# First-layer recurrence: scores ahead of the key transposes, fillers dropped, keys and two joins moved from VectorE to ScalarE

## The reference, cut to what matters

```
z = p[..., (2 + d) * A_WIDTH:(3 + d) * A_WIDTH]
f = max(lb[d] + (1 - lb[d]) * sigmoid(z), F_MIN)
log_f = log(f);  k = 1 - f
# per chunk:
b = cumsum(gc)
decay[t, s] = exp(min(b[t] - b[s], 0)) where s <= t, else 0
scores = einsum('bhtk,bhsk,bhtsk->bhts', qc, kc, decay)
out = (q * exp(b)) @ state + scores @ v
new_state = exp(b_last) * state + (k * exp(b_last - b)).T @ v
```

## Time and profile before

| | before |
|---|---|
| median of 3 runs | 2728.24 us (2727.13 to 2730.35) |
| the profiled execution's own time | 2725.84 us |
| its span, first to last instruction | 2724.0 us |
| TensorE busy in the span | 2551.5 us (94%) |
| VectorE busy | 1672.8 us (61%) |
| ScalarE busy | 992.0 us (36%) |
| mean granted TensorE clock | 0.986 of full speed |

### The profile page before, as it was taken

One profiled execution on the slowest core, in us unless ns is written; L12 is line 12 of the kernel. 1 busy time (PEld: TensorE's weight loads), 2 busy tenths in 40 slices (PEclk: granted clock), 3 DMA queues, 4 the chain that ended last, 5 costly groups with the idle time before them and its releaser, 6 DMA issues. The chain is left out here.

```text
span 2724.0 us, 36802 instructions
## 1 busy us (share of the span) xinstructions
PE 2551.5 (94%) x14963; PEld 2155.6 (79%) x14963; DVE 1672.8 (61%) x2730; ACT 992.0 (36%) x1361; POOL 86.9 (3%) x132
## 2 busy tenths in 40 slices
PE   7999988999999999988999999998989988989997
PEld 2888877888888888866679989976678886767786
DVE  4888875457677766544446756746666775354744
ACT  4226544432211222344344323324542223434632
POOL 0110000000000000000000000002100000000000
PEclk9999999999999999999999999999999999999999
DMA  6650002223344333221013443321220001211232
GB/s 237 192 165 26 17 16 78 80 76 93 99 147 127 100 107 103 78 70 49 1 55 116 132 155 121 121 84 54 78 72 16 16 9 39 97 55 66 76 103 85
DMA packets 62106, 232.28 MB, mean 85 GB/s; under 512 B 6897, under 2 KB 9585, under 8 KB 61298
## 3 DMA queue, kind: packets, MB, share of 16 engines
q1 hardware_dynamic: 46962, 175.40, 19.5%
q0 software_dynamic: 14976, 54.53, 6.4%
HBM read 227.02 MB, written 2.10 MB: 84 GB/s over the span
## 5 line engine op out<-in xcount | busy, mean ns | idle before, releaser
L378 DVE TENSOR_TENSOR w_lo<-w_raw,w_hi 128x1024 fp32r<-128x1024 f32 (+4 forms) x284 | 348.7, 1228 | 376.1 <-ACT w_hi L337 370.6
L337 ACT ACTIVATE w_hi<-w_raw 128x1024 fp32r<-128x1024 f32 (+4 forms) x284 | 297.8, 1049 | 222.7 <-PE late_acc L459 93.4
L459 PE MATMUL mid_acc<-mid_h_hi,w_hi 128*128 128x258 f32 x832 | 279.4, 336 | 1.5 <-DVE mid_od_fq L627 1.0
L459 PE MATMUL mid_acc<-mid_h_hi,w_lo 128*128 128x258 f32 x832 | 279.0, 335 | 0.0
L459 PE MATMUL mid_acc<-mid_h_lo,w_hi 128*128 128x258 f32 x832 | 277.1, 333 | 0.0
L459 PE MATMUL late_acc<-late_h_hi,w_hi 128*128 128x258 f32 x704 | 199.3, 283 | 0.0
L459 PE MATMUL late_acc<-late_h_hi,w_lo 128*128 128x258 f32 x704 | 198.4, 282 | 0.0
L459 PE MATMUL late_acc<-late_h_lo,w_hi 128*128 128x258 f32 x704 | 197.7, 281 | 0.0
L459 PEld LDWEIGHTS mid_acc<-mid_h_hi,w_hi 128*128 128x128 f32 x832 | 157.3, 189 | 19.3 <-issue 2.4
L459 PEld LDWEIGHTS mid_acc<-mid_h_lo,w_hi 128*128 128x128 f32 x832 | 157.5, 189 | 18.6 <-issue 1.2
L459 PEld LDWEIGHTS mid_acc<-mid_h_hi,w_lo 128*128 128x128 f32 x832 | 156.8, 189 | 16.1
(11 more groups left out here) (552 smaller groups left out, 6126.6 us busy)
## 6 DMA issues: line engine op xcount, KB each, us to landing
w_raw<-in_up SPq DMA_DIRECT2D x88, 512.0 KB, 3.6
mid_side_raw<-in_ada_t POOLq DMA_DIRECT2D x48, 512.0 KB, 3.9
w_raw<-in_down SPq DMA_DIRECT2D x32, 704.0 KB, 4.0
qvz_side_raw<-in_ada_t POOLq DMA_DIRECT2D x32, 512.0 KB, 4.5
w_raw<-in_dn_qkv SPq DMA_DIRECT2D x25, 512.0 KB, 3.3
late_side_raw<-in_ada_t POOLq DMA_DIRECT2D x24, 512.0 KB, 4.2
w_raw<-in_da SPq DMA_DIRECT2D x18, 512.0 KB, 3.3
w_raw<-in_ev_qvz SPq DMA_DIRECT2D x16, 512.0 KB, 4.3
```

The lines of the kernel that those rows point to most:

```text
L337: nc.scalar.activation(K.whi[:, g % 2, 0:width], K.raw[:, g % 2, 0:width], ACT.Copy).then_inc(K.hi_done, 1)
L378: nc.vector.tensor_tensor(K.wlo[:, g % 2, 0:width], K.raw[:, g % 2, 0:width], K.whi[:, g % 2, 0:width].bitcast(F32), ALU.subtract).then_in ...
L459: last = nc.tensor.matmul(self.acc[i % len(self.acc)][:, at:at + width], left[:, j, cols], right[k][:, moving:moving + width], start=(k == ...
```

## The change

Four things change, all in the class `Recurrence`:

- On TensorE `turn_keys` goes from ahead of the scores (turn 5) to behind `base_scores` (turn 7), and `BUSY_KEYS` keeps only the 10 fillers of unit 0.
- On ScalarE `keys_back` goes from turn 6 to turn 7, behind a new stage `place`, which writes the parts of the two largest joins (128 and 64) into `S` by three plain copies; `merge` on VectorE keeps the two small joins and the base part.
- The keys `1 - f` are made by ScalarE at the head of `log`, from a bias of ones, and no longer by VectorE.
- On VectorE `update` stands ahead of `both`.

```diff
-    BUSY_KEYS = {0: 10, 4: 18, 5: 2, 7: 18, 8: 2, 9: 9, 10: 8, 11: 8}
+    PLACED = 2
+    MERGES = len(JOINED) - PLACED + 1
+
+    BUSY_KEYS = {0: 10}
...
-        def keys(n):
-            if n >= 2:
-                dve.wait_ge(self.mixed, n - 1)
-            nc.vector.tensor_scalar(self.heads(self.k[n % 2]), self.of_z(n), -1.0, 1.0,
-                                    ALU.mult, ALU.add).then_inc(self.k_done, 1)
...
-            if n >= 2:
-                dve.wait_ge(self.o_done, n - 1)
-            for l, size in enumerate(JOINED):
-                if l % 2 == 0:
-                    dve.wait_ge(self.scored, 3 * n + l // 2 + 1)
-                if l:
-                    dve.wait_ge(self.merged, 5 * n + l)
+            dve.wait_ge(self.placed, n + 1)
+            dve.wait_ge(self.scored, 3 * n + 2)
+            for l in range(self.PLACED, NL):
+                size = JOINED[l]
+                if l > self.PLACED:
+                    dve.wait_ge(self.merged, self.MERGES * n + l - self.PLACED)
...
-        yield from self.turns({0: [(0, merge)], 1: [(1, decayed_base)], 2: [(1, decayed)], 3: [(3, keys)],
-                               4: [(0, both), (0, update)], 5: [(2, base_and_ends)], 6: [(2, levels)], 7: [(3, sums)]})
+        yield from self.turns({0: [(0, merge)], 1: [(1, decayed_base)], 2: [(1, decayed)],
+                               4: [(0, update), (0, both)], 5: [(2, base_and_ends)], 6: [(2, levels)], 7: [(3, sums)]})
...
         def log(n):
+            if n >= 2:
+                act.wait_ge(self.mixed, n - 1)
+            nc.scalar.activation(self.heads(self.k[n % 2]), self.of_z(n), ACT.Identity, scale=-1.0,
+                                 bias=self.K.ones[:, 0:1]).then_inc(self.k_done, 1)
             act.wait_ge(self.k_done, n + 1)
             nc.scalar.activation(self.of_z(n), self.of_z(n), ACT.Ln).then_inc(self.logged, 1)
...
+        def place(n):
+            d = n % 2
+            if n == 0:
+                act.wait_ge(self.zeroed, 1)
+            if n >= 2:
+                act.wait_ge(self.o_done, n - 1)
+            act.wait_ge(self.scored, 3 * n + 1)
+            for l in range(self.PLACED):
+                size = JOINED[l]
+                nb, h = CHUNK // size, size // 2
+                late, early = self.late(d, size)
+                out = self.heads(self.S[d]).rearrange("p h (n e) -> p h n e", e=size)
+                at = l * A_HEADS * (CHUNK // 2)
+                got = self.ps_s[0][:, at:at + A_HEADS * (CHUNK // 2)].rearrange("p (h n e) -> p h n e", h=A_HEADS, e=h)
+                for m in range(nb):
+                    keys = slice(m * size + early.start, m * size + early.stop)
+                    last = nc.scalar.activation(out[keys, :, m, late], got[keys, :, m, :], ACT.Copy)
+            last.then_inc(self.placed, 1)
...
-                               6: [(1, keys_back)]})
+                               6: [(1, place)], 7: [(1, keys_back)]})
...
             if n:
-                pe.wait_ge(self.merged, 5 * (n - 1) + 2 * half + 2)
+                if half == 0:
+                    pe.wait_ge(self.placed, n)
+                else:
+                    pe.wait_ge(self.merged, self.MERGES * (n - 1) + NL - self.PLACED)
...
-        yield from self.turns({2: [(0, read_out)], 3: [(0, gain)], 5: [(1, turn_keys), (1, lambda n: scores(n, 0))],
-                               6: [(1, lambda n: scores(n, 1))], 7: [(1, base_scores)]})
+        yield from self.turns({2: [(0, read_out)], 3: [(0, gain)], 5: [(1, lambda n: scores(n, 0))],
+                               6: [(1, lambda n: scores(n, 1))], 7: [(1, base_scores), (1, turn_keys)]})
```

More of the change, by code:

```diff
@@ L1115, in __init__ @@
          self.mixed, self.scored, self.merged, self.k_turned, self.kt_done, self.o_done, self.o_taken, self.u_done,
-         self.updated) = K.signals("gl", "loaded zeroed k_done logged summed related grown ends mixed scored merged "
-                                   "k_turned kt_done o_done o_taken u_done updated")
+         self.updated, self.placed) = K.signals(
+             "gl", "loaded zeroed k_done logged summed related grown ends mixed scored merged "
+             "k_turned kt_done o_done o_taken u_done updated placed")
     SLOTS = range(-3, 12)
-    BUSY_KEYS = {0: 10, 4: 18, 5: 2, 7: 18, 8: 2, 9: 9, 10: 8, 11: 8}
+    PLACED = 2
+    MERGES = len(JOINED) - PLACED + 1
+    BUSY_KEYS = {0: 10}
     def at(self, n):
@@ L1263, in merge @@
             dve.wait_ge(self.scored, 3 * n + 3)
-            dve.wait_ge(self.merged, 5 * n + NL)
+            dve.wait_ge(self.merged, self.MERGES * n + NL - self.PLACED)
             nc.vector.copy_predicated(self.heads(S), self.mask[d][NL].unsqueeze(1).to_broadcast([P, H, CHUNK]),
@@ L1335, in read_out @@
             d = n % 2
-            pe.wait_ge(self.merged, 5 * n + 5)
+            pe.wait_ge(self.merged, self.MERGES * (n + 1))
             pe.wait_ge(self.mixed, n + 1)
```

## The result

| | before | after |
|---|---|---|
| median of 4 runs, same chip | 2727.68 us (2725.21 to 2730.35) | 2752.32 us (2751.41 to 2756.18) |
| ratio after to before, 95% interval | | 1.0096 [1.0081, 1.0112] |
| profiled execution, its span | 2725.84, 2724.0 us | 2751.83, 2750.0 us |
| TensorE, VectorE, ScalarE busy | 2551.5, 1672.8, 992.0 us | 2563.2, 1657.7, 1009.0 us |
| mean granted TensorE clock | 0.986 | 0.975 |

The account below looks back on a forecast made before the run. No engine fills the stage, so waits bound it; a serial loop through ScalarE replaces waits and fillers. Ten units -1 us, start +4, tail -0.8: net about +2.5, so 2731 us, range 2716 to 2744.

Parts of the forecast that it names:

- TensorE's clock: Without fillers TensorE waits at the scores and slows: 2 us each for units 7 and 10, 1.7 start, 1.5 tail.
- the walk: Unit-by-unit ordering of some hundred steps of three engines with estimated durations; half a microsecond error a unit is 6 us.
- Rival 4: Every TensorE wait of 3 us or more, six in all, costs 3.4 us of clock: 2744 us, chance 0.16.
- The loop: Scores, base product, key transposes, `keys_back`, exponentials, `decayed` in series: 13.8 us a unit, 190 for ten with what stands between.
- rival 2: Loop as forecast, but without 9 us of late TensorE and 6 of clock: 2716 us, chance 0.18.
- soft terms: In the loop, TensorE late at scores or held at a mix transpose, 9 us; and the clock, 6 us.
- signs of the loop: No waits on `update`, 15 to 30 us for `decayed`, `decayed` ends 190 to 196 apart, stage 244 to 250 us.
- Start and tail: Ahead of and behind the ten units: start net +4.0 us against 15.3, tail net -0.8 against 15.3, clock included.
- ScalarE's copies: The three small join copies on ScalarE: 0.9 us a unit, between 0.6 and 1.8; as load they cost nothing.
- VectorE's relief: VectorE loses two masked copies and the keys per unit, 15 us over the stage, but this is not paid out.
- rival 3: The loop through ScalarE does not bind; 39 us less the start's 4 are gained: 2693 us, chance 0.04.
- Rival 5: ScalarE hands on `w_hi` and the mix late, TensorE waits, 0.7 us more a unit: 2739 us, chance 0.12.

Follow-up runs that it names:

- first kernel: Changed kernel with fillers put ahead of TensorE's waits for `decayed` (units 0 and 7 to 11): 2733.02 us, ratio 1.0023 to the kernel before.
- eleventh: Changed kernel with fillers in TensorE's waits for `decayed` and also for the mix: 2732.87 us, ratio 1.0023 to the kernel before.
- tenth kernel: Changed kernel with fillers behind the wait for `decayed`, ahead of the scores of units 7, 10 and 11: 2759.90 us, ratio 1.0119 to the kernel before.
- second: Changed kernel with `turn_keys` and `keys_back` back at their old turns, fillers of units 4 to 11 still out: 2716.41 us, ratio 0.9968 to the kernel before.
- third: Kernel before with its fillers of units 4 to 11 taken out, nothing else changed: 2726.83 us, ratio 1.0000.
- eighth: Kernel before without fillers of units 4 to 11, only key transposes and `keys_back` moved as in the change: 2757.43 us, ratio 1.0111.
- fourth kernel: Changed kernel with only `keys_back` moved on ScalarE, behind the next unit's exponentials: 2719.54 us, ratio 0.9971 to the kernel before.

## Why the prediction was wrong

**The step that failed is the term "TensorE's clock".** It counted 2 us for units 7 and 10, 1.7 at the start, 1.5 for the tail, with 3.4 as the upper end of each. The intervals between the ends of `decayed` in the changed kernel, less the shorter of the first and eleventh kernels' at the same place (same order, waits filled), give it the size below. Here and in the next paragraph the sum is over such best places, which no one kernel has together: both kernels still have slow stretches (27 and 20 us in all, one in each tail).

| place | forecast for the clock | after | shorter of the two | lost to the clock |
|---|---|---|---|---|
| start, unit 0 to 1 | 1.7 | 23.3 | 18.8 | 4.5 |
| unit 7 to 8 | 2 | 19.8 | 14.7 | 5.2 |
| unit 9 to 10 | 0 | 25.7 | 20.9 | 4.8 |
| unit 10 to 11 | 2 | 19.8 | 14.7 | 5.1 |
| tail | 1.5 | 20.1 | 15.2 | 4.9 |
| sum | 7.2 | | | 24.5 |

The 17 us between the sums are most of the 21 by which the median missed. Whole kernels, without any choice of places, say it more carefully: the first kernel gets 19.3 us back with 27 us of slow clock left, 12 more than the forecast had for the clock.

Two things were wrong in the term. First, a slow stretch was taken to be 6.8 us long, as the one in the earlier trace rows, whatever runs in it. That one had 36 rows of fillers in it. At units 7 and 10 the slow stretches are 6.8 us long, all four, where fillers stand behind the wait (the tenth kernel and the kernel before, 36 rows each, 16 in unit 10 of the kernel before), and 10.0 to 17.1 with work alone (the changed kernel, the second, third and eighth). In unit 7 the 11.0 us from scores to transposes are all slow; half of that is 5.5, and 5.2 were lost. Second, a wait of 3 us was taken to leave the clock alone, from the one row of 2.99 us; the third kernel's row of the same length, and the 2.24 us of unit 9, where 4.8 us were lost and none forecast, speak against it. Of the waits themselves the walk had all the long ones, and one of 4 to 6 us in unit 3 that did not come. **Rival 4**, the clock at every long wait, was the closest at 2744 and had the mechanism; with 3.4 us for each wait it too was too cheap, since the five waits cost 4.5 to 5.2 each. Its sign, more than 20 us of the stage at 1.2 GHz, came at 81, and the kernel before had 20 already.

**The loop was right in its path, and its size somewhat short.** Over the best places the ten units take 193.5 us; the walk had 190. Unit 0 to 1 takes 18.8 (19.1 in the forecast without clock), the tail 15.2 (13.0). So the loop itself was 5 us short, which is the rest of the miss to within 2 us, and rival 2, without the soft terms, falls. In one kernel it is more: the ten units take 202.1 us in the first and 198.9 in the eleventh, part of it in slow stretches that the changed kernel doesn't have, such as 24.5 us for unit 4 to 5 in the first against 19.9. The signs of the loop came: no wait on `update`, 23.0 us of waits for `decayed`, `keys_back` the longest wait, some 27 us of VectorE's waits for the exponentials. Those of its length did not: 209.1 for 190 to 196, and 269.8 for a stage of 244 to 250. The first kernel, at nearly the clock that the kernel before had (0.95, 0.96), is 6 us slower than before; the forecast, with its 7 us for the clock, had 2.5.

**Start and tail.** Unit 0's `decayed` ends 17.1 us into the stage, 1.3 earlier than before, for 1.4 in the forecast. With the clock, the start costs a net 6.7 in place of 4.0, and the tail 4.9 more than before in place of 0.8 less.

**ScalarE's copies.** The three of `place` took 0.94 in the row shown (0.9 was taken, between 0.6 and 1.8). Its order and not its load was what counted, as forecast: the fourth kernel gains 33 us from one copy's turn. **VectorE's relief** was not paid out in the change, whose loop binds (rival 3 falls), but the moves, with `update` ahead, are worth 3 to 10 us where the keys stay first. **Rival 5**: TensorE's waits for the mix's norm grew from the earlier trace rows's 2.0 to 3.9, those for its squares from 1.7 (L1495 of the kernel before) to 4.9, and filling them gave nothing in the eleventh; it had no share that can be told apart.

**Fillers.** The forecast let 20 us go with them from TensorE's path. Taken out of the kernel before alone they give 0.0 (interval -2.7 to +2.5 us): a gain of about the fillers' time, all of it paid for the clock. Summed by parts, medians by the ratios: fillers out 0, the order +30, ScalarE's and `update`'s moves -4, together the +26 of the change. Open is `update` ahead of `both`, which was not tried by itself.

## What to carry to other kernels

A filler belongs ahead of the wait, into a free bank, and cut to end with it: there it cost next to nothing and held TensorE's clock (22 us here with nothing else changed); behind the wait it paid back no more than it cost (nothing gained in the kernel before, 8 us lost in the tenth). An order that lets TensorE start early but puts the product that another engine needs last can close a loop over all engines; follow it once around before the waits that it removes are counted as won. And price a slow stretch by work that was seen running in it, since dummy products ended it sooner here, and don't take one row in which the clock held for a rule.

## What the hardware did that was not expected

TensorE could be busy without a gap and stay at 1.2 GHz. Behind the 6.29 us wait of the changed kernel it was busy, by the profile, for 13.10 of 13.10 us at a clock of 0.51, and in the kernel before without fillers for 14.60 of 14.60 us, with scores, transposes and projections. Behind the same wait of 6.29 us, 128x128 fillers had it back after 3 us. The Trainium skill, TensorE: Matmul & The Clock Gate, section "What's actually happening", says that "activity releases the throttle"; the trace agrees for the fillers and does not for these 13 us of gapless rows. The same kind of work was slow for only 6.8 us behind the third kernel's wait of 2.99 us, so the work alone does not fix the length either. Which property of a product counts there was not tried. The other surprise is that a us at 1.2 GHz cost only 0.24 to 0.36 us of the kernel's time in all the pairs where filled waits took it away: a part of the slow products lies beside other engines' work.
